# Attention values one unit later in the TensorE block, weight sums in other VectorE slots, and a copy between two sigmoids

## What is computed

```python
h = rmsnorm(x, g_mix_pre)
proj = h @ w_in                      # q, k, v, conv inputs, two gates
q = rope(q), k = rope(k)
a = window_attention_prompt(q, k, v, sinks)   # 4 blocks of 128 queries, 16 heads, window 128
merged = sigmoid(ga + b0) * (a @ w_attn_branch) + sigmoid(gb + b1) * (b_out @ w_conv_branch)
x = x + rmsnorm(merged @ w_o, g_mix_post)
...
```

## Time and profile before

| | |
|---|---|
| median of 3 runs | 2754.64 us |
| the profiled execution, its own time | 2751.71 us |
| its span in the profile | 2749.7 us |
| TensorE matmul busy | 2693.4 us (98%) |
| TensorE weight load busy | 2618.8 us (95%) |
| VectorE busy | 2252.3 us (82%) |
| ScalarE busy | 1404.6 us (51%) |
| DMA | 357.86 MB, mean 130 GB/s |

### The profile page before, as it was taken

The page is one execution under the profiler, slowest core; times in us unless marked ns, Lnnn a source line. Parts: engine busy times, 40 slices in busy tenths (PEclk is TensorE's granted clock), DMA queues, the critical chain, the costliest instruction groups (busy, mean ns, idle before and its releaser), DMA issues. The chain is left out here.

```text
span 2749.7 us, 55332 instructions
## 1 busy us (share of the span) xinstructions
PE 2693.4 (98%) x21139; PEld 2618.8 (95%) x21139; DVE 2252.3 (82%) x3960; ACT 1404.6 (51%) x2501; POOL 30.3 (1%) x52
## 2 busy tenths in 40 slices
PE   8999999999999999999999999999999999999799
PEld 7999999999999999989999999999998999989699
DVE  6888888777754488889888888888888888889998
ACT  5445455666652245545555555555554453445354
POOL 0000000000000000000000000000000000000000
PEclk9999999999999999999999999999999999999999
DMA  5333333333354422543323333233334243233553
GB/s 206 132 116 117 109 115 113 118 128 120 126 178 138 165 85 100 182 170 108 134 103 130 112 110 131 103 135 106 114 127 166 95 154 120 97 116 127 183 198 119
DMA packets 119154, 357.86 MB, mean 130 GB/s; under 512 B 13097, under 2 KB 37297, under 8 KB 116384
## 3 DMA queue, kind: packets, MB, share of 16 engines
q1 hardware_dynamic: 116944, 350.19, 36.3%
q0 software_dynamic: 2048, 5.68, 0.7%
HBM read 311.74 MB, written 45.32 MB: 130 GB/s over the span
## 5 line engine op out<-in xcount | busy, mean ns | idle before, releaser
L976 PE MATMUL pair<-o_hi,v_hi 128*128 128x260 f32 x5898 | 1680.8, 285 | 22.5 <-DVE v_lo L1747 8.9
L976 PE MATMUL pair<-o_hi,v_lo 128*128 128x260 f32 x5898 | 1665.8, 282 | 0.0
L1124 ACT ACTIVATE v_hi<-s_raw 128x512 fp32r<-128x512 f32 (+1 forms) x1352 | 839.6, 625 | 995.6 <-PE pair L976 813.8
L976 PE MATMUL pair<-lo,v_hi 128*128 128x260 f32 x4228 | 1195.6, 283 | 0.0
L1747 DVE TENSOR_TENSOR v_lo<-s_raw,v_hi 128x512 fp32r<-128x512 f32 (+1 forms) x1352 | 917.5, 682 | 321.8 <-ACT v_hi L1124 282.7
L976 PEld LDWEIGHTS pair<-o_hi,v_hi 128*128 128x128 f32 x5898 | 1109.6, 188 | 46.3 <-issue 25.4
L976 PEld LDWEIGHTS pair<-o_hi,v_lo 128*128 128x128 f32 x5898 | 1111.9, 189 | 0.0
L976 PEld LDWEIGHTS pair<-lo,v_hi 128*128 128x128 f32 x4228 | 795.4, 188 | 0.4
L976 PE MATMUL pair<-lo_E,v_hi 128*128 128x260 f32 x844 | 238.7, 283 | 0.0
L976 PE MATMUL pair<-lo_A,v_hi 128*128 128x260 f32 x826 | 232.9, 282 | 0.0
L1124 ACT ACTIVATE v_hi<-s_one 128x512 fp32r<-128x512 f32 (+1 forms) x218 | 136.0, 627 | 183.3 <-PE pair L976 177.5
(11 more groups left out here) (210 smaller groups left out, 2197.8 us busy)
## 6 DMA issues: line engine op xcount, KB each, us to landing
s_raw<-in_sstream SPq DMA_DIRECT2D x472, 512.0 KB, 4.8
s_raw<-in_sstream SPq DMA_DIRECT2D x32, 384.0 KB, 3.4
f_scr<-fo SPq DMA_DIRECT2D x88, 130.0 KB, 1.8
g_scr<-d_h SPq DMA_DIRECT2D x16, 520.0 KB, 2.7
g_in<-g_scr SPq DMA_DIRECT2D x32, 260.0 KB, 2.7
x_scr<-y_sb SPq DMA_DIRECT2D x8, 1040.0 KB, 4.4
raw<-f_scr SPq DMA_DIRECT2D x7, 1040.0 KB, 4.7
raw<-in_x SPq DMA_DIRECT2D x4, 1040.0 KB, 6.9
```

The source lines that it names most:

```text
L976: mm = pe.matmul(out, wt[:, slot, kk * P:kk * P + P], r[:, k, :], start=j in (0, 1, 3) and k == 0 and n == 0, stop=k == nk - 1 and n == 2, ...
L1124: nc.scalar.activation(v_hi[:, n % 4, 0:width], src, ACT.Copy).then_inc(v_hi_rdy, 1)
```

## The change

It does five things. (1) `values(n)` moves from between products 2 and 3 of unit TURN to the head of the block before the products of the unit behind that (table VALUE), ahead of the transposes of step n+1 and the scores of step n+2; its output goes to bank 0 instead of bank 2, so it waits for the masking that read bank 0, and the scores wait for the copy of the step before last. In unit 31 the values of steps 14 and 15 stay inside the unit. (2) The copy `attention_out` moves with it, to the start of ScalarE's unit. (3) In all units with attention, VectorE does s1 of the next unit at slots 0 and 1, and s4 and s3 at slot 3: the first half of s4 and both of s3 ahead of the split of half 7, the second half of s4 behind it. (4) The first copy (r1) of a unit stands between the two sigmoids instead of behind both. (5) The waits of the first two branch steps are adapted.

```diff
@@ -53,6 +53,7 @@
 TURN = {u + 1: n for u, n in ATT.items() if u != LAST}
+VALUE = {u + 1: n for u, n in TURN.items() if u != LAST}
@@ -807,6 +808,7 @@
                     pe.wait_ge(m_ready, n)
+                    pe.wait_ge(a_rdy, max(n - 1, min(n, 2)))
@@ -819,7 +821,7 @@
                 pe.wait_ge(prob_ready, n + 1)
                 if n:
-                    pe.wait_ge(a_rdy, n)
+                    pe.wait_ge(pT_out, 2 * n)
@@ -830,9 +832,12 @@
             def values(n):
                 blk = n // 4
                 pe.wait_ge(pT_out, 2 * n + 2)
+                pe.wait_ge(m_ready, n + 1 if n < 2 else min(n + 2, 16))
+                if n:
+                    pe.wait_ge(a_rdy, n)
...
-                        mm = pe.matmul(bank[2][HD * g:HD * g + HD, 0:256],
+                        mm = pe.matmul(bank[0][HD * g:HD * g + HD, 0:256],
@@ -849,12 +854,12 @@
-                if u in TURN or u in ATT:
-                    here[-1] = lambda: (turn(TURN[u]) if u in TURN else None,
+                if u in TURN or u in ATT or u in VALUE:
+                    here[-1] = lambda: (values(VALUE[u]) if u in VALUE else None,
+                                        turn(TURN[u]) if u in TURN else None,
                                         scores(ATT[u]) if u in ATT else None)
-                if u in TURN:
+                if u == LAST:
                     here[2] = lambda: values(TURN[u])
-                if u == LAST:
                     here[4] = lambda: turn(ATT[u])
                     here[5] = lambda: values(ATT[u])
@@ -1029,8 +1034,9 @@
                 if isinstance(m, int) and m == 0:
                     pe.wait_ge(m_ready, 16)
+                    pe.wait_ge(a_rdy, 16)
                 elif isinstance(m, int) and m == 1:
-                    pe.wait_ge(a_rdy, 16)
+                    pe.wait_ge(pT_out, 32)
@@ -1194,6 +1200,8 @@
                 n = s_of(u, 0)
+                if u in VALUE:
+                    attention_out(VALUE[u])
                 for i in range(14):
@@ -1321,8 +1329,8 @@
-                if u and kind(u - 1) == "g" and i in (0, 1):
-                    sigmoid_g(u - 1, i)
+                if u and kind(u - 1) == "g" and i == 0:
+                    sigmoid_g(u - 1, 0)
@@ -1337,6 +1345,8 @@
                     copied(u, 2, d[:, 0, HALF:T], r2_out)
+                if u and kind(u - 1) == "g" and i == 1:
+                    sigmoid_g(u - 1, 1)
@@ -1345,7 +1355,7 @@
-                if u in TURN and i == 7:
+                if u == LAST and i == 7:
                     attention_out(TURN[u])
@@ -1764,6 +1774,8 @@
+                if u and u - 1 not in PLAIN:
+                    dve.wait_ge(s2_done, 2 * (u - 1 - earlier(u - 1)) + h + 1)
@@ -1919,9 +1931,17 @@
+                attends = u in ATT or u in TURN or u in VALUE
+                follows = u != U_O - 1 and u + 1 not in PLAIN
                 for i in range(14):
                     if i in first:
                         evac(u, i)
+                    if attends and follows and i in (0, 1):
+                        s1(u + 1, i)
+                    if attends and i == 3:
+                        s4(u, 0)
+                    if attends and follows and i == 3:
+                        both_halves(s3, u + 1)
                     if (u, i // 2, i % 2) in place and s_of(u, i // 2, i % 2) + 4 < n + ahead:
                         v_low(s_of(u, i // 2, i % 2) + 4)
...
+                    if attends and i == 3:
+                        s4(u, 1)
                     i4, i1, i3 = (2, 5, 8) if is_second(u) else (4, 8, 10)
-                    if i in (i4, i4 + 1):
+                    if not attends and i in (i4, i4 + 1):
                         s4(u, i - i4)
-                    if i in (i1, i1 + 1) and u != U_O - 1 and u + 1 not in PLAIN:
+                    if not attends and follows and i in (i1, i1 + 1):
                         s1(u + 1, i - i1)
-                    if i in (i3, i3 + 1) and u != U_O - 1 and u + 1 not in PLAIN:
+                    if not attends and follows and i in (i3, i3 + 1):
                         s3(u + 1, i - i3)
```

More of the change, by code:

```diff
@@ L1294, in attention_out @@
                 nc.scalar.activation(a_st[n % 2][:, :, :],
-                                     bank[2][:, 0:256].rearrange("p (v s) -> p v s", v=2),
+                                     bank[0][:, 0:256].rearrange("p (v s) -> p v s", v=2),
                                      ACT.Copy).then_inc(a_rdy, 1)
```

## The result

The changed kernel takes 2762.95 us, median of 8 runs (2761.3 to 2763.89); the kernel before, on the same chip, 2754.49 (8 runs, 2752.1 to 2754.7). The ratio is 1.0032, 95% interval 1.0022 to 1.0042: slower by some 8.5 us, with 2763 forecast. The profiled execution took 2762.80 us by its own time; its span is 2760.2 us and its mean granted clock 0.995.

A forecast was written before the change was run, and what follows sets the result against it. TensorE, 98% busy, bounds the kernel, so only its idle moments count. Steady unit +1.11 - 0.61 = +0.50 us, +5.5 over 11; other units bring +8.6 in all: 2763 on the median, range 2753 to 2770.

The forecast's parts named there:

- Half 8 is pinned by ScalarE at S + 12.98, gain of the values' leaving 0: Steady unit, S its first product matmul: ScalarE's chain sets half 8's start, so taking 1.21 us of values away gains 0.
- the rival that the values only change places: TensorE's arrival, not ScalarE, sets half 8; moving values is free, waits go, unit 23.4 us, whole 2743; chance 0.15.
- Head +1.11: Values at the head of a steady unit's block have nothing to hide them: +1.11 us, bounds 0.87 and 1.21.
- Scores' wait free with 0.4 us of cover in steady units, 1.65 into the block in unit 18: Scores wait for the values' copy, ready near 1.65 us; transposes cover it until 2.08, but unit 18 has none: +1.6.
- The rival in which the scores wait in every unit: Copy 0.8 us later than taken, cover gone, 12 heads pay 0.4 more: +5 us, 2768; chance 0.08.
- Sums: half 7 late by 0.9 inside the pin, waits at half 11 and product 6 gone, -0.61: Steady unit: three sums delay half 7 by 0.9 us, costing 0 before half 8; two later waits go, -0.61 us.
- r1 copy 0: The r1 copy, 0.6 us sooner, only shortens the stretch before half 8 that ScalarE's chain pins: 0.
- Second mask late and harmless: Unit 20: second mask issued 3.3 us in, landing 4.6 later, 1.0 to 1.2 us behind the masking wanting it; cost 0.
- Conv units and unit 18: +1.2, 0 and +2.3, 3.5 together: Unit 15 gains a head, +1.2 us; units 14 and 17 net 0; unit 18 net +2.3 from scores, half 8, waits.
- Unit 31 +0.2: Unit 31: values 13 on top, +1.1 us; transposes of step 15 no longer wait, -0.9; net +0.2.
- Within 0.2%: Rival: heads at their lower bound, 0.87 - 0.61 = +0.26 us in 11 units, and +1: 2757 to 2759; chance 0.22.
- The rival of the clock: Waits of 1.4 us a unit lower TensorE's clock; each unit loses about 0.2 to 1.7 us: 2765 to 2782; chance 0.02.

The follow-up runs named there:

- b1: Kernel before the change, with only the r1 copy moved between the two sigmoids; 2754.3 us, ratio 0.9999.
- a1: Changed kernel with VectorE's sums in their old slots and the r1 copy behind both sigmoids, so only the values, their copy and waits move; 2766.94 us.
- b4: Changed kernel with the three sums of slot 3 behind the low part of half 7 instead of ahead of it; 2768.75 us.
- a2: Kernel before, with only the sums in their new slots and the r1 copy between the sigmoids; values stay behind product 2; 2748.6 us.
- a3: Changed kernel with Exp in place of Sigmoid for the gates of units 18 to 30, so no table loads there (output wrong); 2744.93 us.
- a4: a2 with the r2 copy and the high part of half 8 ahead of the exponentials in units 18 to 31; 2744.35 us.

## Why the prediction was right

- **Half 8 is pinned by ScalarE at S + 12.98, gain of the values' leaving 0**: right, and the heart of it. Half 8 starts at S + 12.98 in b1, at S + 12.99 in the change, a1 and b4 and at S + 13.00 in a2, though TensorE would be there between 0.15 us (b1, a2) and 1.2 us (a1) sooner; a3 takes away two table loads, a4 moves the exponentials, and the pin is gone in both. With it the rival that the values only change places falls: it wanted a unit of 23.4.
- **Head +1.11**: measured +1.16. The values' own 1.02 and the 0.09 ahead of them came out as taken, but the transposes now take 1.02 to the scores instead of 0.97. This is the term that makes the steady unit +0.55 instead of +0.50, 0.6 us over 11 units.
- **Scores' wait free with 0.4 us of cover in steady units, 1.65 into the block in unit 18**: right; the copy of the values ends 1.53 us into the block of unit 23 and the scores start at 2.04, and in unit 18 they start at 1.67. The rival in which the scores wait in every unit falls with that.
- **Sums: half 7 late by 0.9 inside the pin, waits at half 11 and product 6 gone, -0.61**: right. The low part ends at S + 10.9, the wait is 0.88, and b4 shows that it costs nothing in a steady unit. The list of what would be seen said that TensorE stands 0.9 "again" before half 8; it is 0.38 over a normal step, as S + 12.5 to S + 12.98 in the working gives.
- **r1 copy 0**: right (b1). **Second mask late and harmless**: the cost of 0 is right, the lateness did not come. It was issued at 489.80, 3.2 us into unit 20 as forecast, but the two mask loads landed in 2.8 and 4.0 us in this execution instead of 4.6, and the first masking of unit 20 stands at S + 3.02, as that of unit 23 does (S + 3.01). So no run shows what a late mask would have cost.
- **Conv units and unit 18: +1.2, 0 and +2.3, 3.5 together**: 3.81 measured for the stretch with unit 19's block. By their parts, unit 15 with its head is +1.2, units 14 and 17 are +0.07 each, the head of unit 18 +1.7 and the rest of unit 18 +0.75. In unit 18 there was a wait of 1.12 at half 7 that the working did not name, and half 8 started at S + 13.27 for 13.15.
- **Unit 31 +0.2**: its new head is in the 6.56 of the row before it, and the rest is -0.95 for -0.9.
- **Sum +8.6**: 9.4 in the stretch that the terms cover, 8.5 between the medians. The terms were short by 0.8, and that the median agrees to 0.1 is chance. The forecast for the profiled execution, 2760.3, was 2.5 short of its 2762.80: 0.8 by the terms, the rest outside the stretch, where the change's execution happened to be longer.
- **Within 0.2%**: this rival wanted heads at their lower bound, 0.87; with 1.16 it has no ground left.
- **The rival of the clock** got little chance, and its mechanism did not act in this stretch of the change: its steady unit has a granted clock of 1.00, with waits of 0.88 and 0.38 us in it. The row with 1.00 that the working names there is unit 23 of before, whose waits come to 0.61 by its own sum; no row shown is of a unit that waits 0.9. b4 shows that the loss lay nearer than I thought, in waits of 1.9 us.
- **The Trainium skill on the table switch** (ScalarE: Activation LUTs, What ACT_TABLE_LOAD costs), 2.66 us with the drain: a3 gives 1.40 for one switch, so by this kernel the row decides, and the pin is where the row put it.

## What to carry to other kernels

When an engine's work stands in front of an instruction that another engine pins, that work is free where it is, and moving it out of there costs its full length; find the pin (an instruction whose start keeps its distance from the unit's start when the work ahead of it changes) before moving anything. A pin that is taken away shows the next one, one half or one bank further on (half 8, half 9, product 6 here), so the edits pay only together: late exponentials alone gave +0.13 us a unit, the sums (with the r1 copy) alone -0.60, all together -0.82. And an order of slots that fits one kind of unit is to be costed again for each other kind: the sums' new slots won 0.6 in plain gate units and lost 1.9 in the conv stretch.

## What the runs showed of the hardware that I had not expected

A wait's price can be more than its length. In b4 two waits of 1.88 and 1.89 us were each followed, about 1 us after TensorE had started again, by some 3.3 us at 1.2 GHz; the change itself has the same pattern later in the program, behind waits of 2.08 us (2295.99) and 1.96 us (2460.63). Windows of the changed kernel there, and behind a wait of 2.24 us (2604.92):

```profile
2296.50:2299.50 3.00, 3.00 (x19) 3.00 (x18) 3.00 (x7) 0.63 (x1) 0.00 (x0) 0.60 0.54 169
2461.00:2464.00 3.00, 3.00 (x16) 3.00 (x15) 2.97 (x8) 0.53 (x1) 0.00 (x0) 0.50 0.38 131
2605.50:2607.50 2.00, 2.00 (x19) 2.00 (x18) 2.00 (x3) 2.00 (x3) 0.00 (x0) 1.00 0.69 283
```

The last row, at full clock behind the longest of these waits, keeps it from being a matter of the wait's length alone. Nor is it a matter of the instructions around the wait: the kernel before has the wait of 2295.99 too, at the same place of the same program, and there the clock stayed at 1.00 (timeline of PE and window of the kernel before):

```profile
2286.99 0.39 PE L976 MATMUL pair<-o_hi,v_hi 128*128 128x260 f32 x1 [2.09 <-DVE y_sb L1996]
2287.50:2290.50 3.00, 3.00 (x25) 2.94 (x25) 3.00 (x7) 0.96 (x2) 0.00 (x0) 1.00 0.56 172
```

From this wait to the next one, which brought the clock down in both, the change takes 164.64 us and the kernel before 163.13: the 1.5 us that such a fall costs. So the same wait costs them in one execution and not in another, and two profiles of one kernel can differ by that much. What decides was not tried. The Trainium skill (TensorE: Matmul & The Clock Gate, A second HAM failure mode: psum-queue depth-cycling) tells of a clock that goes up and down by short idle times between groups of matmuls; here waits of up to 1.2 us in each of 11 units left it at 1.00, and falls in this stretch stood only behind the two single waits of b4.

Eight transposes take 1.02 to 1.03 us to the scores behind them when values stand ahead, and 0.96 to 0.97 when products do, in unit 23 of every kernel here. A cause was not tested.
